# Strassen steps for both products of an MLP, in two passes with the activations in DRAM

## Chip, cores and metric

The kernel runs on one core of one Trainium2 chip. The metric is the device time of one execution in microseconds (us), as the median of a few runs. A profiled execution of the kernel before lies under the readings below.

## What is computed

Two transformer blocks over 1024 tokens of width 1024, in fp32. The change touches the end of the second: the last product with `w_out`, the norm, and the MLP.

```python
D_MODEL = 1024; SEQ = 1024; D_FF = 4 * D_MODEL
...
        x = x + jnp.einsum('bsd,de->bse', merged, w_out)

        h2 = rms_norm(x, norm2_g)
        u = jnp.square(jax.nn.relu(jnp.einsum('bsd,df->bsf', h2, w_up)))
        x = x + jnp.einsum('bsf,fd->bsd', u, w_down)
```

## The kernel before

TensorE takes fp32r operands, so every fp32 operand is split into a high part (a copy to fp32r) and a low part (the operand less its high part). A product is then three passes, high by high, high by low and low by high (`three_passes`, L202 issues all matmuls). The splits are work of the other engines: ScalarE (ACT) writes high parts, VectorE (DVE) the low parts of activations, GpSimd (POOL) the low parts of weights.

Each phase is a block with its own instruction stream for each engine, written out by hand and held together by semaphores; all engines pass a barrier between two blocks. There is no scheduler: every engine takes its instructions in the order of the code, and one that waits holds up all behind it. `phase_norm("n3", ...)` makes the last product with `w_out`, adds the residual into `res`, norms each of the 8 token tiles, turns it (transposes on TensorE) and leaves the turned rows in `a_hi` and `a_lo` (feature by token). Two halves of the first MLP units are also done there (`fm_half`).

`phase_mlp` takes the 4096 hidden features in 8 groups of 512. Of each group, `up` makes the four tiles of 128 features (8 k-tiles by two token halves by three passes, 48 matmuls of 128x512 each). ACT applies relu and square (`evacuate`) into `mlp_u`. The product with `w_down` of the group is one Strassen step: 512 rows of `w_down` by 1024 columns in four quadrants, and seven products `m1` to `m7` in place of eight. DVE makes the sums of activations (`total`, L2335) and their low parts (L2324), POOL the sums of weights (`combine`, L2147) and their low parts (`low`, L2154), ACT the high parts (`high` L2259, `w_part` L2262). A product has 4 token tiles of 6 matmuls, and DVE adds each tile from PSUM (`ps`) to one or two places of the residual in `res` (`add`, L2342). Products of one group and `up` tiles of the next are interleaved on TensorE:

```python
                        product(i, "m3", count("m3"), None if first else i * 28 - 4)
                        if not last:
                            pe.wait_ge(w_ready, ready(i, "up0"))
                            up(i + 1, 0)
                        product(i, "m4", count("m4"), i * 28)
                        product(i, "m5", count("m5"), i * 28 + 4)
```

All of `mlp_u` stays in SBUF. The weights of the next group are loaded by SP as soon as POOL has made the last low part that reads the buffer (`load_down`, `load_up`).

Of the kernel before, what the change touches and what calls it, by code (L numbers as in the profile page):

```python
# [13 lines left out]
P = 128  # L14
T = 1024
# [39 lines left out]
def program(nc, io, out):  # L55
    ctx = ExitStack()
    with ctx:
# [10 lines left out]
        x1 = dram("x1_tm", (T, D))  # L68
        qkv2 = dram("qkv2_tm", (T, 3072))
# [137 lines left out]
        n_mm_l, n_out_l, n_mm_r, n_prepared = (Tally(sem(n)) for n in ("n_mm_l", "n_out_l", "n_mm_r", "n_prepared"))  # L207
        n_added, n_normed, n_turned = (Tally(sem(n)) for n in ("n_added", "n_normed", "n_turned"))
# [1134 lines left out]
        def phase_norm(name, out_start, opened, x_src, gain, post_gain=None, x_dst=None, next_dst=None, next_col=0):  # L1343
# [12 lines left out]
            stored = n_stored if x_dst is not None else None  # L1356
            with ExitStack() as mem, nc.Block() as block:
# [11 lines left out]
                gain_in, chain, squared = S("gain_in"), S("chain"), S("squared")  # L1369
                rooted = S("rooted")  # L1370
# [119 lines left out]
                def _(act):  # L1490
                    passed = [0]

                    def square(src, total):
                        if passed[0]:
                            act.wait_ge(squared, passed[0])
                        nc.scalar.activation(junk[:, 0:src.shape[-1]], src, ACT.Square, accum_out=total).then_inc(squared, 1)
                        passed[0] += 1

# [55 lines left out]
                def _(dve):  # L1554
# [63 lines left out]
                    else:  # L1618
# [5 lines left out]
                        for s in range(NT + 1):  # L1624
                            if s < NT:
                                right_add(s)
                                pre_norm(s)
                            if s:
                                low(s - 1)

            for tally, n in ((n_hi, NT), (n_lo, NT), (n_mm_l, 2 * NT), (n_out_l, NT), (n_mm_r, NT), (n_prepared, NT),
# [410 lines left out]

        def phase_mlp():
# [11 lines left out]
            start = W_MLP[0][0]  # L2055
            u0, c0 = fm_units[0], tm_chunks[0]
            GROUPS = 8
            PRODUCTS = ("m3", "m4", "m5", "m2", "m1", "m6", "m7")
            STEPS = ("m3", "up0", "m4", "m5", "up1", "m2", "m1", "m6", "m7", "up2", "up3")
            QUARTER = {"up2": 0, "up3": 1, "m3": 2, "up0": 3, "m4": 0, "m5": 1, "up1": 2, "m2": 3, "m1": 0, "m6": 1, "m7": 2}  # L2060
            ADDS = {"m1": ((0, 0, ALU.add), (1, 1, ALU.add)), "m2": ((1, 0, ALU.add), (1, 1, ALU.subtract)),
                    "m3": ((0, 1, ALU.add), (1, 1, ALU.add)), "m4": ((0, 0, ALU.add), (1, 0, ALU.add)),
                    "m5": ((0, 0, ALU.subtract), (0, 1, ALU.add)), "m6": ((1, 1, ALU.add),), "m7": ((0, 0, ALU.add),)}
            OPERANDS = [("m3", 0), ("m3", 1)] + [(p, 0) for p in ("m4", "m5", "m2", "m1", "m6", "m7")] + \
                       [(p, 1) for p in ("m4", "m5", "m2", "m1", "m6", "m7")]
            SUMS = [(p, k) for k in range(2) for p in ("m5", "m2", "m1", "m6", "m7")]

            def tiles(p):
                return 4 * PRODUCTS.index(p)

            with ExitStack() as mem, nc.Block() as block:
                ut = sb(mem, "mlp_u", [P, 4, T])
                uo_hi = sb(mem, "mlp_uo_hi", [P, 7, 2, 512], F32R)
                uo_lo = sb(mem, "mlp_uo_lo", [P, 7, 2, 512], F32R)
                raw_b = sb(mem, "mlp_raw_b", [P, KB // 2, 512])
                raw_x = sb(mem, "mlp_raw_x", [P, 2, 512])
                raw_a = halved(w_raw)
                squared, u_hi, u_lo, summed = sem("mlp_squared"), sem("mlp_u_hi"), sem("mlp_u_lo"), sem("mlp_summed")
                a_in, b_in, x_in = sem("mlp_a_in"), sem("mlp_b_in"), sem("mlp_x_in")
                combined, w_high, w_ready = sem("mlp_combined"), sem("mlp_w_high"), sem("mlp_w_ready")  # L2080
                mm_d, ev_d = sem("mlp_mm_d"), sem("mlp_ev_d")

                r11, r21, r12, r22 = raw_a[:, 0:2, :], raw_a[:, 2:4, :], raw_b[:, 0:2, :], raw_b[:, 2:4, :]
                raw_of = {"m3": r12, "m4": r21, "m5": r22, "m2": r11, "m1": r22, "m6": r12, "m7": r21}

                def quarter(side, step):
                    q = QUARTER[step]
                    return halved(side[slot_of(start + 1 - q // 2)])[:, q % 2 * 2:q % 2 * 2 + 2, :]

                def by_k(tile):  # L2090
                    return tile.rearrange("p a (b n) -> p (a b) n", n=P)

                def u_part(p, k):

                    unit = k if p in ("m3", "m6", "m2") else 2 + k
                    half = 0 if p in ("m3", "m5", "m7") else 1
                    return ut[:, unit, half * 512:(half + 1) * 512]

                def ready(i, step):
                    return i * len(STEPS) + (STEPS.index(step) + 1)  # L2100

                def ready_last(step):
                    return (GROUPS - 1) * len(STEPS) + (PRODUCTS.index(step) + 1)

# [7 lines left out]
                def _(sp):  # L2112
                    def load_down(i, c):
                        rows = io["w_down_2"][i * 512:(i + 1) * 512, c * 512:(c + 1) * 512].rearrange("(k p) n -> p k n", p=P)
                        sp.dma_start((raw_b if c else raw_a)[:, :, :], rows).then_inc(b_in if c else a_in, 16)

                    def load_up(i, q):
                        col = i * 512 + q * P
                        sp.dma_start(by_k(raw_x[:, :, :]),
                                     io["w_up_2"][:, col:col + P].rearrange("(k p) n -> p k n", p=P)).then_inc(x_in, 16)  # L2120

                    load_down(0, 1)
                    for i in range(GROUPS - 1):
                        if i:
                            sp.wait_ge(w_ready, ready(i - 1, "up3"))
                        load_up(i + 1, 0)
                        sp.wait_ge(w_ready, ready(i, "up0"))
                        load_up(i + 1, 1)
                        sp.wait_ge(w_ready, ready(i, "up1"))
                        load_up(i + 1, 2)  # L2130
                        sp.wait_ge(w_ready, ready(i, "m7"))
                        load_down(i + 1, 1)
                        load_down(i + 1, 0)
                        sp.wait_ge(w_ready, ready(i, "up2"))
                        load_up(i + 1, 3)
                    for r, c, p in ((0, 1, "m5"), (1, 0, "m2"), (1, 1, "m6"), (0, 0, "m7")):
                        for t in range(4):
                            sp.wait_ge(ev_d, (GROUPS - 1) * 28 + tiles(p) + t + 1)
# [319 lines left out]
```

## Time and profile before

| quantity | before |
|---|---|
| median of 3 runs | 2311.85 us (2310.8 to 2312.58) |
| profiled execution, own time | 2313.34 us |
| its span, first to last instruction | 2311.6 us |
| mean granted TensorE clock | 0.993 of full |
| TensorE busy | 2233.6 us, 97% |
| GpSimd busy | 941.1 us, 41% |
| VectorE busy | 1319.2 us, 57% |
| ScalarE busy | 802.0 us, 35% |

Busy shares say how much of the span an engine had an instruction in work. A matmul's own duration in the trace overlaps its neighbours', so the pace is read from the distance of starts. Idle time in brackets names the engine or transfer that ended it.

### The profile page before, as it was taken

To read this page: it belongs to the slowest core of one execution; us is meant where nothing else is said; L and a number is where in the kernel's file an instruction comes from. 1 tells how busy PE (TensorE), PEld (TensorE's weight loads), DVE (VectorE), ACT (ScalarE), POOL (GpSimd) and SP (SyncE) were. 2 spreads that over 40 slices of the span, in tenths; PEclk is the share of its full clock that TensorE was granted. 3 is DMA by queue.
4 is the path that set the end of the run, shared out by engine and by line. 5 is a ranking of instruction groups with operands and counts; after the bars stand their busy time and mean duration, and the time that the engine had idled before them with its cause. 6 is when DMAs were issued, how large, how long until landed. Compare 5 with 4: busy or idle time off the path is not lost. (4 is left out here: it accounts for less than half of the span.)

```text
span 2311.6 us, 30049 instructions
## 1 busy us (share of the span) xinstructions
PE 2233.6 (97%) x10722; PEld 1854.4 (80%) x10722; DVE 1319.2 (57%) x2544; ACT 802.0 (35%) x1491; POOL 941.1 (41%) x732
## 2 busy tenths in 40 slices
PE   7999989999999999999999999999999999999997
PEld 7778777778877888888888788888888888888886
DVE  6666674516444666666666582334365565556467
ACT  5444424200004555555554131212333323323322
POOL 3232445535542322313313364553356355554534
PEclk9999999999999999999999999999999999999999
DMA  6220114212324323323322472222110110110211
GB/s 216 94 75 19 42 55 162 83 65 89 111 97 132 107 79 92 100 66 104 87 82 83 164 254 92 92 100 92 55 55 28 64 63 18 64 64 22 68 46 73
DMA packets 177605, 199.79 MB, mean 86 GB/s; under 512 B 56360, under 2 KB 126536, under 8 KB 177520
## 3 DMA queue, kind: packets, MB, share of 16 engines
q1 hardware_dynamic: 100352, 122.47, 16.1%
q10 hardware_dynamic: 77168, 76.19, 10.6%
q8 instruction: 53, 0.87, 0.2%
q14 instruction: 32, 0.26, 0.0%
HBM read 156.63 MB, written 50.40 MB: 90 GB/s over the span
## 5 line engine op out<-in xcount | busy, mean ns | idle before, releaser
L157 POOL TENSOR_TENSOR w_hi<-w_raw,zero 128x512 fp32r<-128x512 f32 x224 | 271.3, 1241 | 967.3 <-PE ps L202 847.5
L202 PE MATMUL ps<-a_hi,w_hi 128*128 128x512 f32 x1664 | 606.7, 405 | 7.4 <-PEq L1654 3.3
L202 PE MATMUL ps<-a_hi,w_lo 128*128 128x512 f32 x1664 | 586.8, 393 | 0.0
L202 PE MATMUL ps<-a_lo,w_hi 128*128 128x512 f32 x1664 | 584.7, 392 | 0.0
L202 PEld LDWEIGHTS ps<-a_hi,w_lo 128*128 128x128 f32 x1664 | 313.8, 189 | 69.3
L202 PEld LDWEIGHTS ps<-a_hi,w_hi 128*128 128x128 f32 x1664 | 314.8, 189 | 62.5 <-issue 9.2
L202 PEld LDWEIGHTS ps<-a_lo,w_hi 128*128 128x128 f32 x1664 | 315.2, 189 | 53.4
L2342 DVE TENSOR_TENSOR res<-res,ps 128x512 f32<-128x512 f32 x384 | 244.7, 682 | 118.0 <-PE ps L202 108.6
L162 POOL TENSOR_TENSOR w_lo<-w_raw,w_hi 128x512 fp32r<-128x512 f32 x224 | 299.7, 1370 | 4.4
L202 PE MATMUL ps<-w_hi,a_hi 128*128 128x512 f32 (+1 forms) x640 | 245.7, 384 | 7.5 <-PEq L1123 2.2
L202 PE MATMUL ps<-w_hi,a_lo 128*128 128x512 f32 (+1 forms) x640 | 244.1, 381 | 0.0
L202 PE MATMUL ps<-w_lo,a_hi 128*128 128x512 f32 (+1 forms) x640 | 244.0, 381 | 0.0
L202 PE MATMUL ps<-w_hi,mlp_uo_hi 128*128 128x512 f32 x448 | 179.1, 400 | 8.2 <-issue 5.4
L2324 DVE TENSOR_TENSOR mlp_uo_lo<-mlp_u,mlp_uo_hi 128x512 fp32r<-128x512 f32 x112 | 89.1, 829 | 160.8 <-ACT mlp_uo_hi L2259 159.1
L202 PE MATMUL ps<-w_lo,mlp_uo_hi 128*128 128x512 f32 x448 | 178.8, 399 | 0.0
L202 PE MATMUL ps<-w_hi,mlp_uo_lo 128*128 128x512 f32 x448 | 178.7, 399 | 0.0
L1894 ACT ACTIVATE prob<-prob,st 128x640 f32<-128x640 f32 (+4 forms) x128 | 89.3, 697 | 223.9 <-DVE st L2003 223.0
L202 PEld LDWEIGHTS ps<-w_hi,a_hi 128*128 128x128 f32 x640 | 121.7, 190 | 31.9 <-issue 7.5
L2154 POOL TENSOR_TENSOR w_lo<-w_raw,w_hi 128x512 fp32r<-128x512 f32 x48 | 62.5, 1324 | 203.1 <-ACT w_hi L2262 202.7
L202 PEld LDWEIGHTS ps<-w_hi,a_lo 128*128 128x128 f32 x640 | 121.9, 190 | 23.1
L202 PEld LDWEIGHTS ps<-w_lo,a_hi 128*128 128x128 f32 x640 | 121.9, 191 | 22.8
L532 DVE COPY stage_tm<-ps 128x512 f32<-128x512 f32 x40 | 27.7, 692 | 152.0 <-PE ps L202 152.0
(206 smaller groups left out, 3301.9 us busy)
## 6 DMA issues: line engine op xcount, KB each, us to landing
w_raw<-in_w_in_dram SPq DMA_DIRECT2D x32, 1024.0 KB, 5.2
feat_fm<-stage ACTq DMA_DIRECT2D x68, 256.0 KB, 2.1
mlp_raw_x<-in_w_up_dram SPq DMA_DIRECT2D x28, 512.0 KB, 4.1
conv_in<-feat_fm ACTq DMA_DIRECT2D x24, 512.0 KB, 5.8
qkv_tm<-stage_tm ACTq DMA_DIRECT2D x5, 2048.0 KB, 6.9
res<-in_x_dram SPq DMA_DIRECT2D x16, 512.0 KB, 6.4
w_raw<-in_w_out_dram SPq DMA_DIRECT2D x8, 1024.0 KB, 5.0
qk_raw<-qkv_tm ACTq DMA_DIRECT2D x32, 256.0 KB, 3.9
```

The costliest lines, as they stand in the source:

```text
L157: hi = nc.gpsimd.tensor_tensor(w_hi[slot][:, k:k + 2, :], w_raw[:, k:k + 2, :], zero[:, 0:1].unsqueeze(2).to_broadcast([P, 2, CW]), ALU.add)
L162: lo = nc.gpsimd.tensor_tensor(w_lo[slot][:, k:k + 2, :], w_raw[:, k:k + 2, :], w_hi[slot][:, k:k + 2, :].bitcast(F32), ALU.subtract)
L202: last = nc.tensor.matmul(out_of(o), lhs, rhs(o), start=first and n == 0, stop=final and n == 2)
L532: nc.vector.tensor_copy(stage[:, q, t, :], ps[:, t, 0:width]).then_inc(ev_tm, per)
L1894: nc.scalar.activation(prob[:, s, 0:w], prob[:, s, 0:w], ACT.Exp, scale=-1.0, bias=st[:, s, 1:2], accum_out=st[:, s, 2:3]).then_inc(exped, 1)
L2154: last = nc.gpsimd.tensor_tensor(quarter(w_lo, step)[:, k, :], raw[:, k, :], quarter(w_hi, step)[:, k, :].bitcast(F32), ALU.subtract)
L2324: nc.vector.tensor_tensor(uo_lo[:, int(p[1]) - 1, k, :], u_part(p, k), uo_hi[:, int(p[1]) - 1, k, :].bitcast(F32), ALU.subtract).then_inc( ...
L2342: last = nc.vector.tensor_tensor(rows, rows, ps[:, 4 + t, :], op)
```

## The change

The MLP becomes two passes. First all 8 groups of `w_up` are done, each as one Strassen step (seven products of 2 tiles by 12 matmuls, `up_tile`); the partial results are put together in `mlp_acc` by ACT (copies) and DVE (adds), ACT applies relu and square, and a DMA writes them to `u_fm` in DRAM. The residual also passes through DRAM (`x2`). Then the product with `w_down` is done in 4 groups of 1024 hidden features, seven products of 4 tiles by 12 matmuls each, in the order m5, m3, m2, m1, m6, m4, m7. The activation quadrants of a product are loaded from `u_fm`, summed by DVE and split two products ahead of their use. The seven operands of the first pass are made once: two are parts of the normed rows, two are differences made in the new `phase_norm_last`, three are sums made by POOL there.

The new phase between the product with `w_out` and the MLP, at each token tile t:

```diff
+                    for t in range(4, NT):
+                        pool.wait_ge(n_hi.sem, hi0 + t + 1)
+                        toks = slice((t - 4) * P, (t - 3) * P)
+                        nc.gpsimd.tensor_tensor(raw_c[:, :, toks], turned_row(t - 4, 0), turned_row(t, 4), ALU.add).then_inc(p_sum, 1)
+                        nc.gpsimd.tensor_tensor(turned_row(t - 4, 4), turned_row(t - 4, 4), turned_row(t, 4), ALU.add).then_inc(p_sum, 1)
+                        pool.wait_ge(u_sum, t + 1)
+                        nc.gpsimd.tensor_tensor(turned_row(t, 0), turned_row(t, 0), turned_row(t - 4, 0), ALU.add).then_inc(p_sum, 1)
...
+                    def low(t):
...
+                        nc.vector.tensor_tensor(diff[:, t % 2, :, :], turned_row(t, k0), turned_row(t, k1), ALU.subtract).then_inc(u_sum, 1)
...
+                    for s in range(NT + 2):
+                        if s < NT:
+                            right_add(s)
+                            pre_norm(s)
+                        if 1 <= s <= NT:
+                            low(s - 1)
+                        if s >= 2:
+                            diff_low(s - 2)
```

The first pass on TensorE, one product:

```diff
+        def up_tile(p, fb, last=False):
...
+            for k in range(4):
+                mm = three_passes(lambda _: ps[:, 2 * UP_PLACE[p] + fb, :], wh[:, k, cols], wl[:, k, cols],
+                                  lambda _: high[:, k, :], lambda _: low[:, k, :], (0,), k == 0, k == 3)
```

The second pass, SP (loads of weights), POOL, TensorE, ACT and DVE in turn; `s` counts the 28 products:

```diff
+                        if p == "m6":
+                            sp.wait_ge(w_ready, NU + s + 1)
+                            load_down(g, 1, 0)
...
+                            if p == "m7":
+                                sp.wait_ge(combined, down_sum(s))
+                                load_down(g + 1, 1, 1)
+                                sp.wait_ge(w_ready, NU + s + 1)
+                                load_down(g + 1, 0, 1)
...
+                    for s in range(ND):
+                        g, p = s // 7, DOWN[s % 7]
...
+                        if p == "m1":
+                            pool.wait_ge(a_in, 16 * GROUPS + 16 * (g + 1))
+                            down_total(r1, r1, r2, ALU.add)
+                        if p == "m6":
+                            pool.wait_ge(combined, down_sum(s) - 1)
+                            down_total(r0, r0, r1, ALU.add)
+                        if p == "m4":
+                            pool.wait_ge(b_in, 16 * GROUPS + 32 * g + 32)
+                            down_total(r0, r0, r2, ALU.subtract)
...
+                        pool.wait_ge(w_high, NU + s + 1)
+                        for k in range(4):
+                            ins = nc.gpsimd.tensor_tensor(down_slot(w_lo, s)[:, k, :], raw_of[p][:, k, :],
+                                                          down_slot(w_hi, s)[:, k, :].bitcast(F32), ALU.subtract)
+                        ins.then_inc(w_ready, 1)
...
+                    for s in range(ND):
+                        pe.wait_ge(w_ready, NU + s + 1)
+                        pe.wait_ge(u_lo, SPLIT_UP + 4 * s + 4)
...
+                        for t in range(4):
...
+                                pe.wait_ge(ev_p, 8 * GROUPS + 4 * (s - 2) + t + 1)
+                            toks = slice(t * P, (t + 1) * P)
+                            for k in range(4):
+                                mm = three_passes(lambda _: ps[:, 4 * (s % 2) + t, :], high[:, k, toks], low[:, k, toks],
...
+                    for s in range(ND):
+                        if s + 1 < ND:
+                            act.wait_ge(mm_p, NU + 4 * s)
+                            down_high(s + 1)
+                        if s + 2 < ND:
+                            staged_high(s + 2)
...
+                    for s in range(ND):
+                        if s + 2 < ND:
+                            staged_sum(s + 2)
...
+                        for t in range(4):
+                            down_add(s, t)
+                            if s + 2 < ND and t < 2:
+                                staged_low(s + 2, (2 * t, 2 * t + 1))
```

`down_total` and `staged_sum` are four `tensor_tensor` of 128x512, `down_high` is two copies of 128x1024, `staged_high` and `staged_low` are four instructions of 128x512. `down_high` of five of the seven products waits for `combined`, which `down_total` raises; the weight parts alternate between two slots.

**POOL, the last group's weights.** In the program of before, in the last group of 512 features, the low parts for m3, m4 and m5 stand together, and then the sums for m1, m6 and m7 (x2 is two instructions alike):

```order
L2154 TENSOR_TENSOR w_lo1<-mlp_raw_b,w_hi1 128x512 [waits mlp_w_high]
L2154 TENSOR_TENSOR w_lo1<-mlp_raw_b,w_hi1 128x512
L2154 TENSOR_TENSOR w_lo0<-w_raw,w_hi0 128x512 [waits mlp_w_high]
L2154 TENSOR_TENSOR w_lo0<-w_raw,w_hi0 128x512
L2154 TENSOR_TENSOR w_lo0<-mlp_raw_b,w_hi0 128x512 [waits mlp_w_high]
L2154 TENSOR_TENSOR w_lo0<-mlp_raw_b,w_hi0 128x512
L2147 TENSOR_TENSOR mlp_raw_b<-w_raw,mlp_raw_b 128x512 x2
L2147 TENSOR_TENSOR mlp_raw_b<-mlp_raw_b 128x512 [waits mlp_combined]
```

In the changed program, in the first group of the second pass, from the sum for m6 to the low part for m7:

```order
L2532 TENSOR_TENSOR mlp_raw_b<-mlp_raw_b,mlp_raw_c 128x512 [waits mlp_combined]
L2532 TENSOR_TENSOR mlp_raw_b<-mlp_raw_b,mlp_raw_c 128x512 x3
L2555 TENSOR_TENSOR w_lo1<-mlp_raw_b,w_hi1 128x512 [waits mlp_w_high]
L2555 TENSOR_TENSOR w_lo1<-mlp_raw_b,w_hi1 128x512 x3
L2532 TENSOR_TENSOR mlp_raw_b<-mlp_raw_b,w_raw 128x512 [waits mlp_b_in]
L2532 TENSOR_TENSOR mlp_raw_b<-mlp_raw_b,w_raw 128x512 x3
L2555 TENSOR_TENSOR w_lo0<-mlp_raw_b,w_hi0 128x512 [waits mlp_w_high]
L2555 TENSOR_TENSOR w_lo0<-mlp_raw_b,w_hi0 128x512 x3
```

A sum and the low part that is made of it now stand directly behind one another, four instructions each, with a wait for ACT (`mlp_w_high`) between them and a wait for a load (`mlp_b_in`) ahead of m4's sum.

**DVE, one product.** Before, a product's adds (two for each token tile), with two low parts of the next group ahead of the next product's adds (register arithmetic left out):

```order
L2342 TENSOR_TENSOR res<-res,ps 128x512 [waits mlp_mm_d]
L2342 TENSOR_TENSOR res<-res,ps 128x512
...
L2324 TENSOR_TENSOR mlp_uo_lo<-mlp_u,mlp_uo_hi 128x512 [waits mlp_u_hi]
```

In the changed program, one product of the second pass with sums two products ahead (`mlp_part_x` and `mlp_part_y` are the loaded quadrants):

```order
L2748 TENSOR_TENSOR mlp_part_y<-mlp_part_x,mlp_part_y 128x512 [waits row_in0]
L2748 TENSOR_TENSOR mlp_part_y<-mlp_part_x,mlp_part_y 128x512 x3
L2799 TENSOR_TENSOR res<-res,ps 128x512 [waits mlp_ev,mlp_mm]
L2799 TENSOR_TENSOR res<-res,ps 128x512
L2753 TENSOR_TENSOR a_lo<-mlp_part_y,a_hi 128x512 [waits mlp_u_hi] x2
```

Four sums now stand ahead of a product's adds and four low parts between them (two behind the first tile's adds, two behind the second's), eight instructions that read two operands in SBUF.

## Rows read from the trace of the kernel before

**Rows 1.** The page, busy time, share of the span and instructions of each engine.

```profile
PE 2233.6 (97%) x10722; PEld 1854.4 (80%) x10722; DVE 1319.2 (57%) x2544; ACT 802.0 (35%) x1491; POOL 941.1 (41%) x732
```

**Rows 2.** Busy us in stretches: PE, PEld, DVE, ACT, POOL, granted clock, DMA share, GB/s.

```profile
1759.00:1841.60 82.60, 82.60 (x361) 67.46 (x360) 48.68 (x72) 27.98 (x33) 42.21 (x32) 1.00 0.16 51
```

**Rows 3.** Line 202 from 1590 us: count, ns min/median/max, first and last start.

```profile
L202 PE MATMUL ps<-a_hi,w_hi x512: 389/389/477, 1631.0 to 2254.6; 128*128 128x512 f32 x171
L202 PE MATMUL ps<-w_hi,mlp_uo_hi x448: 392/394/767, 1676.1 to 2307.1; 128*128 128x512 f32 x150
```

**Rows 4.** The chain that ended last, in order of time: start us, us, what.

```profile
1643.38 612.53 PE ps L202 x2664
...
2264.33 12.99 PE ps L202 x48
...
2278.48 2.96 POOL w_lo L2154 x2
...
2282.68 25.26 PE ps L202 x96
```

**Rows 5.** Timeline of DVE: adds behind 12 matmuls, then behind 6.

```profile
1566.67 0.69 DVE L1560 TENSOR_TENSOR res<-ps,res 128x512 f32<-128x512 f32 x1 [1.94 <-PE ps L202]
...
1569.39 0.69 DVE L1560 TENSOR_TENSOR res<-ps,res 128x512 f32<-128x512 f32 x1 [1.91 <-PE ps L202]
...
1813.15 0.69 DVE L2342 TENSOR_TENSOR res<-res,ps 128x512 f32<-128x512 f32 x1 [0.71 <-PE ps L202]
1814.55 0.69 DVE L2342 TENSOR_TENSOR res<-res,ps 128x512 f32<-128x512 f32 x1 [0.71 <-PE ps L202]
```

**Rows 6.** Groups of instructions, 1759 to 2255 us: count, busy us, mean ns, idle before.

```profile
L2342 DVE TENSOR_TENSOR res<-res,ps 128x512 f32<-128x512 f32 x288 | 183.4, 682 | 94.7 <-PE ps L202 87.9
L2324 DVE TENSOR_TENSOR mlp_uo_lo<-mlp_u,mlp_uo_hi 128x512 fp32r<-128x512 f32 x84 | 68.4, 849 | 109.9 <-ACT mlp_uo_hi L2259 108.7
```

**Rows 7.** Timeline of POOL and DVE from 1788 us, both on SBUF operands.

```profile
1788.05 2.40 DVE L2335 TENSOR_TENSOR mlp_u<-mlp_u 128x512 f32<-128x512 f32 x2
1788.06 3.55 POOL L2154 TENSOR_TENSOR w_lo<-mlp_raw_b,w_hi 128x512 fp32r<-128x512 f32 x2 [3.03 <-ACT w_hi L2262]
...
1790.37 2.39 DVE L2324 TENSOR_TENSOR mlp_uo_lo<-mlp_u,mlp_uo_hi 128x512 fp32r<-128x512 f32 x2
1792.69 1.28 DVE L2335 TENSOR_TENSOR mlp_u<-mlp_u 128x512 f32<-128x512 f32 x2
```

**Rows 8.** Timeline of POOL and DVE from 1766 us, DVE reading PSUM.

```profile
1766.14 4.86 DVE L2342 TENSOR_TENSOR res<-res,ps 128x512 f32<-128x512 f32 x8
...
1768.61 2.56 POOL L2147 TENSOR_TENSOR mlp_raw_b<-w_raw,mlp_raw_b 128x512 f32<-128x512 f32 x2
```

**Rows 9.** Timeline of ACT: two high parts of weights, 128x1024 each.

```profile
2258.63 1.05 ACT L2262 ACTIVATE w_hi<-w_raw 128x1024 fp32r<-128x1024 f32 x1
2259.58 1.04 ACT L2262 ACTIVATE w_hi<-mlp_raw_b 128x1024 fp32r<-128x1024 f32 x1
```

**Rows 10.** Timeline of POOL: a low part, a load into its source, the next high part.

```profile
1556.10 5.04 POOL L162 TENSOR_TENSOR w_lo_n<-w_raw,w_hi_n 128x512 fp32r<-128x512 f32 x4
1566.43 4.03 POOL L157 TENSOR_TENSOR w_hi<-w_raw,zero 128x512 fp32r<-128x512 f32 x4 [5.29 <-DMA w_raw<-in_w_out_dram]
```

**Rows 11.** Busy us in stretches, as rows 2, behind two idle times of TensorE.

```profile
2266.00:2268.00 2.00, 2.00 (x6) 1.62 (x5) 2.00 (x4) 0.00 (x0) 1.92 (x3) 0.51 0.00 0
2284.00:2286.00 2.00, 2.00 (x6) 1.52 (x6) 1.91 (x4) 2.00 (x3) 0.00 (x0) 0.50 0.00 0
```

**Rows 12.** Timeline of DVE in the norm, a token tile's pass.

```profile
1617.62 0.69 DVE L1564 TENSOR_TENSOR res<-ps,res 128x512 f32<-128x512 f32 x1 [1.11 <-PE ps L202]
...
1620.49 1.28 DVE L1599 SCALAR_TENSOR_TENSOR mt_n<-res,stat_n,gpre_n 128x1024 f32<-128x1024 f32 x1
1621.69 1.22 DVE L1604 TENSOR_TENSOR a_lo<-ps,a_hi 128x1024 fp32r<-128x1024 f32 x1
1624.02 0.69 DVE L1564 TENSOR_TENSOR res<-ps,res 128x512 f32<-128x512 f32 x1 [1.11 <-PE ps L202]
```

More of the change, by code:

```diff
@@ L68, in program @@
         x1 = dram("x1_tm", (T, D))
+        x2 = dram("x2_tm", (T, D))
+        u_fm = dram("u_fm", (4 * D, T))
         qkv2 = dram("qkv2_tm", (T, 3072))
@@ L2040, in _ @@
                     pair_loop(dve, body)
-        def phase_mlp():
[L2055 to L2069, printed above, removed]
-            with ExitStack() as mem, nc.Block() as block:
[L2072 to L2103, printed above, removed]
@@ L2143, in _, with up_low @@
                 @block.gpsimd
                 def _(pool):
-                    def combine(dst, a, b, op):
-                        for k in range(2):
+                    def up_low(i, p, last):
+                        pool.wait_ge(w_high, i * 7 + (UP.index(p) + 1))
+                        high, low = up_quarter(w_hi, p, last), up_quarter(w_lo, p, last)
+                        for k in range(0, 4, 2):
+                            ins = nc.gpsimd.tensor_tensor(low[:, k:k + 2, :], up_raw(p)[:, k:k + 2, :],
+                                                          high[:, k:k + 2, :].bitcast(F32), ALU.subtract)
+                        ins.then_inc(w_ready, 1)
@@ L2147, in combine, with body, down_total @@
+                    def body(i, first, last):
+                        for p in UP[2 if first else 0:]:
+                            up_low(i, p, last)
+                    periods(pool, body)
+                    def down_total(dst, a, b, op):
+                        for k in range(4):
                             last = nc.gpsimd.tensor_tensor(dst[:, k, :], a[:, k, :], b[:, k, :], op)
                         last.then_inc(combined, 1)
-                    def low(count, step):
-                        pool.wait_ge(w_high, count)
-                        raw = raw_of.get(step, raw_x)
-                        for k in range(2):
-                            last = nc.gpsimd.tensor_tensor(quarter(w_lo, step)[:, k, :], raw[:, k, :],
-                                                           quarter(w_hi, step)[:, k, :].bitcast(F32), ALU.subtract)
-                        last.then_inc(w_ready, 1)
@@ L2202, in product, with up @@
-                    def product(i, p, count, before):
-                        high, low, o = quarter(w_hi, p), quarter(w_lo, p), int(p[1]) - 1
-                        pe.wait_ge(w_ready, count)
-                        pe.wait_ge(u_lo, i * 14 + (OPERANDS.index((p, 1)) + 1))
+                    def up(i, p, last):
+                        pe.wait_ge(w_ready, i * 7 + (UP.index(p) + 1))
+                        for fb in range(2):
+                            mm = up_tile(p, fb, last)
+                        mm.then_inc(mm_p, 1)
@@ L2254, in high, with up_high @@
[L2254 to L2262 removed]
+                    def up_high(i, p, last=False):
+                        nc.scalar.activation(up_quarter(w_hi, p, last), up_raw(p), ACT.Copy).then_inc(w_high, 1)
@@ L2264, in body, with staged_high @@
+                    def staged_high(s):
+                        if s >= 2 and PARTS[DOWN[s % 7]][1] is None:
+                            act.wait_ge(*staged_in(s))
+                        for k in range(4):
+                            if PARTS[DOWN[s % 7]][1] is not None:
+                                act.wait_ge(u_sum, NT + summed[s] + k + 1)
+                            nc.scalar.activation(down_operand(a_hi, s)[:, k, :], total(s)[:, k, :], ACT.Copy).then_inc(u_hi, 1)
                     def body(i, first, last):
-                        def multiplied(p):
-                            return i * 28 + (tiles(p) + 4)
```

742 lines of the change are left out of this document (539 added, 203 removed).

## The prediction

> **What bounds the kernel now.** I read the page first: TensorE is in work for 97% of the span, POOL for 41% [rows 1]. Then the stretches: in a steady part of the MLP TensorE has no gap at all, DVE is in work for 59% of the time and POOL for 51% [rows 2]. The chain that ended last is one unbroken piece of 2664 matmuls up to the last group; only there do gaps come, where the chain goes over ACT, DVE and POOL [rows 4]. So the MLP is bound by the number of matmuls, and a change pays if it takes matmuls away and the other engines still keep up. The reader should carry both halves of that into what follows.
>
> **Matmuls taken away.** The MLP has 1536 matmuls in the first product and 1344 in the second [rows 3]. Adds behind units of 12 matmuls come 2.72 us apart, 0.2267 us for each matmul; behind 6 with a wait they come 1.40 us apart, so a tile's wait costs about 0.04 us [rows 5]. The first product takes 1536 x 0.2267 = 348.2 us, the second 224 x 1.40 = 313.6 us. The MLP runs from 1631.0 to 2308.0 us [rows 3, 4], 677 us; the rest, some 15 us, is the last turn, a few tenths between phases and the gaps of the last group. The change makes the first product 8 x 7 x 24 = 1344 matmuls, 304.7 us plus 2.2 us of waits = 306.9. The second has 28 products of 4 tiles of 12, at 2.76 us a tile: 11.04 us a product, 77.3 us a group, 309.1 us in all. With 1 us for the last turn that is 617 us, 60 us less than before, if TensorE never waits.
>
> **The first pass** keeps up. A group lasts 38.4 us. POOL has seven low parts of two instructions (about 18 us), DVE eight adds of 128x1024 (1.2 us each, two of the halves in [rows 8]) and five sums of two instructions, 16 us; ACT seven high parts, four copies and eight passes of 128x1024, at 0.95 to 1.05 us [rows 9], 20 us. The tightest step is m4's weights for the next group: their slot is free 5.5 us before the group ends, ACT and POOL need 3.6, and m4 runs 5.5 us into the next. I add nothing. Transfers are 4 MB a group, hidden; without that cover each late load would cost its 5.3 us.
>
> **Two engines on one resource.** Rows 7 decide the rest. DVE and POOL start together on SBUF operands at 1788.05. A DVE instruction that is alone takes 0.6 us (two in 1.28), a POOL one 1.25 (two in 2.56 [rows 8]). Here DVE's first two take 2.40 = 0.6 + 1.8 and the next two 2.39, POOL's two take 3.55 = 0.6 + 1.25 + 0.6 + 1.25 less a tenth: each instruction waits until the other engine's is over, and they alternate [rows 7]. When DVE adds from PSUM, eight take 4.86 us and POOL's two stay at 2.56 [rows 8], so adds don't take part. Over the steady part it shows in the means already, 849 ns for a low part against 682 for an add [rows 6]. The Trainium skill (SBUF — State Buffer, Who interferes with whom) says that a VectorE instruction with two SBUF inputs and a GpSimd one that reads SBUF lock each other out for the whole instruction, and one with a single SBUF input does not. It speaks against this change; by it the sum comes out as it does below from the rows, and if it did not hold, the sum would be that of batches without collisions.
>
> **The second pass.** A product needs four DVE low parts, five of seven four DVE sums: 48 instructions of 0.6 us a group, 28.8 us. POOL makes five sums and seven low parts of four: 48 of 1.25, 60 us. On one resource that is 88.8 us against TensorE's 77.3. But the order binds harder. For a product with a sum POOL does four instructions, ACT two high parts (0.95 each and 0.1 for the signals, 2.0 us [rows 9]), POOL four more, and POOL has nothing else to do while ACT works. For m4 a load into `mlp_raw_b` must also come between m6's low part and m4's sum: 1561.14 to 1566.43 in the same pattern, 5.3 us [rows 10].
>
> I walk one group; time 0 is the end of the preceding m7. POOL's sum for m3 is over at 1.5, its low part at 10.7 (ready for 11.0). m2's weight slot is free when m5 ends at 11.0, so from there the chain runs without slack: high part (2.0), low part m2, sum m1, high, low, sum m6, high, low, load (5.3), sum m4, high, low, sum m7, high, low. That is five high parts, nine batches of four POOL instructions and one load: 10.0 + 5.3 + nine batches. A batch alone is 5.05 us [rows 10]; each DVE instruction between adds 0.6. Stepping both engines by alternation, with DVE's order of sums, add, two low parts, add, two low parts, adds, I get the ends: low m2 19.8, sum m1 27.2, low m1 35.95, sum m6 43.35, low m6 51.5, load 56.8, sum m4 62.5, low m4 71.25, sum m7 78.65, low m7 87.4. So the nine batches take 61.1 us, 6.8 each, and 26 of the group's 48 DVE instructions fall into them. TensorE waits 2.9 us before m1, 4.5 before m6, 8.7 before m4 and 5.1 before m7, which ends at 98.4.
>
> Idle TensorE also loses its clock. Behind gaps of 2.8 and 5.4 us it is granted half, 1.2 instead of 2.4 GHz [rows 11], and 48 and 96 matmuls take 12.99 and 25.26 us instead of 11.2 and 22.4 [rows 4], 1.8 and 2.9 more. Behind m1, m6 and m4 the next wait absorbs this; behind m7 it counts, 2.2 us. The group is 100.6 us, 23.3 more than 77.3. Four groups: 93; the first starts its m3 about 2.5 later, the last has no sums for a following group and saves about 4.5. **+91 us.**
>
> Loads of activations (2 MB a product at most, a product and a half ahead) stay hidden behind the POOL chain; DVE, with 29 us of adds (48 of 0.61) and 29 of sums and low parts a group, plus its waits, lags by up to half a product, which the second PSUM set covers.
>
> **The phase between.** Per token tile DVE is free for 1.1 of 6.4 us now [rows 12]; the change halves `low` (-0.6) and adds two instructions of 0.6, leaving 0.5. POOL works on SBUF meanwhile, first on m2's and m4's weights (17 us), then three sums for each of the last four tiles; each collision costs DVE up to 1.25. I take 1.2 us on the first tiles, 2.2 at tiles 6 and 7. Behind the last turn ACT copies twice (1.7), POOL sums (about 5), the barrier follows, then ACT's high part (1.1) and POOL's low part of m5 (2.6): about 10.6 us, of which m4's 5.4 cover half, so TensorE waits 5.2, plus 2.0 for the clock. **+11 us**, bounds 3 and 16. The queue behind: all ACT copies of the first group follow that high part, with 8 us of slack.
>
> **Sum.** 617 + 11 + 91 = 719 us against 677: +42. The profiled execution would be 2313.3 + 42 = 2355; it lies 1.5 us above the median of 2311.85, so the median becomes 2354 us.
>
> **Rivals.** (A) The collisions hardly happen, because DVE falls into POOL's 15.3 us of waiting per group. Batches are 5.05, the chain 10 + 5.3 + 45.5, the group 82.9 and 2.2 for the clock; four groups +31. 617 + 11 + 31 = 659, 18 less than before: 2294 us, faster. For it: half of DVE's work is adds that don't collide. Against it: 48 instructions cannot fit in 15 us. It decides from below 89.9 us a group, where the time is that of before; that is 5.8 us a batch, some 11 collisions a group in place of 26. (B) POOL's chain isn't on the path at all, and the change gives its matmuls: 617 + 11, 2263 us. Against it is the count of 88.8 us on one resource. (C) Collisions are at their worst, four in each batch, 7.45 us: the group 10 + 5.3 + 67 + 22.1 + 2.2 = 106.7, four +118, total 746: 2381 us; late activation sums would come to the same. (D) Half the collisions, 5.95 a batch: the group 93.2, +64, total 692: 2327 us.
>
> **Numbers.** Forecast 0.52, D 0.14, C 0.13, A 0.12, B 0.04; 0.05 for a time within 0.2% between A and D. 0.2%, 4.6 us, is about what a measurement of this kernel can tell from no change. Faster 0.16 (A and B), same 0.05, slower 0.79. Cases of both signs: the forecast alone would range from 2335 to 2375; the range that leaves out A, B and the far end of C is 2305 to 2385.
>
> **What would show it.** Right: 2688 MLP matmuls; a first pass of about 307 us without gaps; in the second pass POOL near 80% in work, its 128x512 batches near 6.8 us, DVE instructions on `mlp_part` at up to 1.85 us each, groups of about 100 us, gaps on TensorE before m1, m6, m4 and m7 released by POOL's `w_lo`, the longest before m4 with a load of `mlp_raw_b` in it, and a granted clock clearly under 1. Wrong: groups under 90 us with POOL instructions at 1.25 (A), or gaps released by DVE or by loads of `u_fm`, which I take as hidden.

## The result, and the profile after

The changed kernel takes 2334.23 us (median of its four executions), the kernel before, run beside it, 2311.8 us (2310.8 to 2312.58). One of the four, of 4426 us, was disturbed: it is in the median of 2334.23 us but not in the ratio, and the three others took 2333.42 to 2334.99 us, with a median of 2333.48. The ratio is 1.0096, 95% interval 1.0076 to 1.0116: 22.4 us slower, where 42 were forecast. The profiled execution took 2334.99 us.

The head of the page: busy time by engine, share of the span and instructions (answers to [rows 1]).

```profile
span 2333.2 us, 29563 instructions
PE 2199.3 (94%) x10530; PEld 1825.2 (78%) x10530; DVE 1480.9 (63%) x2516; ACT 867.5 (37%) x1577; POOL 1094.8 (47%) x796
```

TensorE has 192 matmuls less and is in work for 34 us less, and the span is 21.6 us longer: 56 us more of idle time came in. Where that lies is told by TensorE's waits from 1500 us on: what it waited for, us in total, times, longest.

```profile
PE ps L204 <- POOL w_lo L2555: 56.4, 15, 8.4
PE ps L204 <- POOL w_lo L2521: 7.8, 2, 7.1
...
```

L2555 is the low part of weights in the second pass, L2521 the one in the first. In the kernel before there was no such wait in a steady stretch [rows 2]. The stretches of the changed kernel, columns as in [rows 2]: the start of the MLP, the first pass, the turn to the second with most of its first group, and two stretches as long as a group in the second.

```profile
1640.00:1655.00 15.00, 7.90 (x23) 6.03 (x22) 10.48 (x7) 10.35 (x15) 13.48 (x9) 0.66 0.00 0
1655.00:1946.00 291.00, 290.28 (x1273) 238.54 (x1273) 189.14 (x153) 152.70 (x157) 153.93 (x107) 1.00 0.39 130
1946.00:2032.50 86.50, 72.79 (x300) 58.60 (x298) 83.20 (x88) 28.77 (x40) 69.11 (x45) 0.92 0.61 218
2032.50:2128.60 96.10, 81.55 (x336) 65.79 (x336) 89.71 (x97) 30.06 (x44) 76.02 (x49) 0.95 0.49 175
2128.60:2224.70 96.10, 81.37 (x336) 65.61 (x336) 87.95 (x97) 29.77 (x43) 76.08 (x49) 0.95 0.50 175
```

The first pass has 0.7 us of gap in 291 at a granted clock of 1.00. In the second pass TensorE is idle for 14.6 us of each 96.1, and its clock is 0.95. The chain that ended last (start us, us, what) shows a whole group of the second pass, from the m7 of one group to that of the next:

```profile
2128.67 22.08 PE ps L204 x96
...
2150.77 2.02 ACT w_hi L2649 x2
...
2152.86 6.40 POOL w_lo L2555 x4
2159.26 7.00 POOL mlp_raw_c L2532 x4
...
2168.43 6.39 POOL w_lo L2555 x4
2174.82 7.00 POOL mlp_raw_b L2532 x4
...
2183.99 5.95 POOL w_lo L2555 x4
...
2189.95 5.24 DMA mlp_raw_b<-in_w_down_dram
...
2195.26 5.63 POOL mlp_raw_b L2532 x4
...
2203.36 6.34 POOL w_lo L2555 x4
2209.70 6.32 POOL mlp_raw_b L2532 x4
...
2218.19 6.52 POOL w_lo L2555 x4
...
2224.76 22.07 PE ps L204 x96
```

Between two pieces of 96 matmuls (m7 and the next group's m5) the chain goes over nine POOL batches, five pairs of ACT high parts (2.0 us each, most left out here) and one load: the chain that the prediction walked, link by link. What is new against it is the length of the batches, 5.6 to 7.0 us with a mean of 6.4, where it had 5.7 to 7.4 with a mean of 6.8. Taken one by one, 26 of the 36 POOL instructions in these nine batches last 1.7 to 1.9 us; the other ten last 1.3.

The timeline of DVE over two of these batches (start us, us, what; in brackets the idle time before):

```profile
2153.15 6.66 DVE L2748 TENSOR_TENSOR mlp_part_y<-mlp_part_x,mlp_part_y 128x512 f32<-128x512 f32 x4
2159.73 1.27 DVE L2799 TENSOR_TENSOR res<-res,ps 128x512 f32<-128x512 f32 x2
2160.93 2.38 DVE L2753 TENSOR_TENSOR a_lo<-mlp_part_y,a_hi 128x512 fp32r<-128x512 f32 x2
2163.23 1.27 DVE L2799 TENSOR_TENSOR res<-res,ps 128x512 f32<-128x512 f32 x2
2164.43 2.38 DVE L2753 TENSOR_TENSOR a_lo<-mlp_part_y,a_hi 128x512 fp32r<-128x512 f32 x2
```

Two adds from PSUM take 1.27 us as before [rows 8]. Two low parts, both operands in SBUF, take 2.38, as in [rows 7], and four sums 6.66 instead of about 2.5. A batch of four POOL instructions that meets four of DVE's takes 7.00 us, one alone 5.05 [rows 10]: a meeting costs POOL 0.49 us, where 0.6 was assumed.

TensorE's clock just behind the gap before m4 (columns as above), and its timeline at the first matmul of m4 and of m7:

```profile
2113.00:2119.00 6.00, 5.32 (x13) 4.17 (x14) 6.00 (x6) 0.00 (x0) 6.00 (x5) 0.50 0.00 0
```

```profile
2113.68 0.80 PE L204 MATMUL ps<-w_hi,a_hi 128*128 128x512 f32 x1 [6.53 <-POOL w_lo L2555]
...
2128.67 0.50 PE L204 MATMUL ps<-w_hi,a_hi 128*128 128x512 f32 x1 [1.25 <-POOL w_lo L2555]
```

Behind the gap of 2.4 us before m1 the 48 matmuls take 11.2 us, the full pace; behind that of 3.9 us before m6 they take 12.8, and behind that of 6.5 us before m4 13.7.

### The profile page after: what moved, and what is told of

Its sections match the earlier page's. It is cut to its first block and busy times, and to the rows that moved or that the text cites. A ratio compares the mean times of both kernels' runs of the same rounds, so it can differ in the third digit from the quotient of the medians.

```text
span 2333.2 us, 29563 instructions
## 1 busy us (share of the span) xinstructions
PE 2199.3 (94%) x10530; PEld 1825.2 (78%) x10530; DVE 1480.9 (63%) x2516; ACT 867.5 (37%) x1577; POOL 1094.8 (47%) x796
## 5 line engine op out<-in xcount | busy, mean ns | idle before, releaser
L204 PE MATMUL ps<-w_hi,a_hi 128*128 128x512 f32 (+1 forms) x1088 | 428.0, 393 | 63.9 <-POOL w_lo L2555 56.4
L204 PE MATMUL ps<-w_lo,a_hi 128*128 128x512 f32 (+1 forms) x1088 | 424.2, 390 | 0.0
L204 PE MATMUL ps<-w_hi,a_lo 128*128 128x512 f32 (+1 forms) x1088 | 424.2, 390 | 0.0
L204 PEld LDWEIGHTS ps<-w_hi,a_hi 128*128 128x128 f32 x1088 | 209.8, 193 | 113.4 <-POOL w_lo L2555 62.8
L204 PEld LDWEIGHTS ps<-w_hi,a_lo 128*128 128x128 f32 x1088 | 209.3, 192 | 42.2
L204 PEld LDWEIGHTS ps<-w_lo,a_hi 128*128 128x128 f32 x1088 | 209.7, 193 | 40.9
L2799 DVE TENSOR_TENSOR res<-res,ps 128x512 f32<-128x512 f32 x192 | 121.4, 675 | 16.7 <-PE ps L204 16.7
L2521 POOL TENSOR_TENSOR w_lo<-mlp_raw_b,w_hi 128x512 fp32r<-128x512 f32 x60 | 85.4, 1446 | 98.2 <-ACT w_hi L2615 98.2
L2019 DVE TENSOR_TENSOR pt_lo<-ps,pt_hi 128x512 fp32r<-128x512 f32 (+1 forms) x192 | 87.9, 485 | 44.8 <-ACT pt_hi L1909 44.8
L2555 POOL TENSOR_TENSOR w_lo<-mlp_raw_b,w_hi 128x512 fp32r<-128x512 f32 x64 | 99.2, 1581 | 36.5 <-ACT w_hi L2649 36.5
L2753 DVE TENSOR_TENSOR a_lo<-mlp_part_y,a_hi 128x512 fp32r<-128x512 f32 x76 | 98.5, 1335 | 22.1 <-ACT a_hi L2658 22.1
```

Source lines behind the costliest of these rows:

```text
L204: last = nc.tensor.matmul(out_of(o), lhs, rhs(o), start=first and n == 0, stop=final and n == 2)
L2019: ins = nc.vector.tensor_tensor(pt_lo[:, sl:sl + cnt, cols], ps[:, bank, 0:cnt * P].rearrange("p (j n) -> p j n", n=P), pt_hi[:, sl:sl + c ...
L2521: ins = nc.gpsimd.tensor_tensor(low[:, k:k + 2, :], up_raw(p)[:, k:k + 2, :], high[:, k:k + 2, :].bitcast(F32), ALU.subtract)
L2555: ins = nc.gpsimd.tensor_tensor(down_slot(w_lo, s)[:, k, :], raw_of[p][:, k, :], down_slot(w_hi, s)[:, k, :].bitcast(F32), ALU.subtract)
L2753: nc.vector.tensor_tensor(down_operand(a_lo, s)[:, k, :], total(s)[:, k, :], down_operand(a_hi, s)[:, k, :].bitcast(F32), ALU.subtract).th ...
L2799: last = nc.vector.tensor_tensor(rows, rows, ps[:, 4 * (s % 2) + t, :], op)
```

## The experiments

Eleven kernels were run in three sets: runs 1 to 4, 5 to 8, and 9 to 11. Beside them the kernel before took 2312.45, 2311.37 and 2313.03 us. Kernels that leave work out were run once, the others four to eight times.

**1. DVE's instructions on SBUF taken away, 2. DVE's adds taken away, 3. POOL's work taken away.** Each is a width of 8 columns in place of 512, in the second pass only. Runs 1 and 3 do the same to the low parts.

```diff
-    nc.vector.tensor_tensor(y[:, k, :], x[:, k, :], y[:, k, :], op)
+    nc.vector.tensor_tensor(y[:, k, 0:8], x[:, k, 0:8], y[:, k, 0:8], op)
...
-    last = nc.vector.tensor_tensor(rows, rows, ps[:, 4 * (s % 2) + t, :], op)
+    last = nc.vector.tensor_tensor(rows[:, 0:8], rows[:, 0:8], ps[:, 4 * (s % 2) + t, 0:8], op)
...
-    last = nc.gpsimd.tensor_tensor(dst[:, k, :], a[:, k, :], b[:, k, :], op)
+    last = nc.gpsimd.tensor_tensor(dst[:, k, 0:8], a[:, k, 0:8], b[:, k, 0:8], op)
```

> In the second pass DVE's sums and low parts of activations work on 8 columns in place of 512, so that the low parts are stale; every wait, ACT, POOL and TensorE stay as they are. Theory (DVE and POOL exclude each other on SBUF operands): POOL's batches of four fall from a mean of 6.4 us to 5.05, the group from 96.1 to 22.1 + 10.9 + 5.3 + 45.5 = 84 us, and the time to about 2286 us. Rival (POOL's batches are long for another reason, ACT's or the transfers' traffic): batches stay at 6.4 us and the time at 2334 us.

> In the second pass DVE's adds from PSUM work on 8 columns in place of 512 (the output is incomplete), sums and low parts stay. Theory: adds with one operand in PSUM take no part in the collisions and DVE is not the bound, so batches stay between 6 and 7 us and the time within 6 us of 2334. Rival 1 (any DVE instruction slows POOL): batches fall, the time falls by 20 us or more. Rival 2 (DVE, in work for 93% of a group, is itself the bound): the group falls from 96 towards 80 us, the time to about 2275.

> In the second pass POOL's sums and low parts of weights work on 8 columns in place of 512 (weights' low parts are stale). Theory: nothing else holds TensorE, 28 products take 309 us in place of 381, and the time is about 2262 us, 50 less than before the change: what the fewer matmuls give less the phase between. Rival (activation loads, ACT or DVE come next behind POOL): gaps remain, the time is 2285 us or more.

Run 1 took 2292.57 us, run 2 2335.68, run 3 2259.88: the theory holds in each, and run 1 lies 7 us above its figure. Run 1's POOL timeline over one load:

```profile
2154.72 5.11 POOL L2555 TENSOR_TENSOR w_lo<-mlp_raw_b,w_hi 128x512 fp32r<-128x512 f32 x4 [2.18 <-ACT w_hi L2649]
2164.93 5.04 POOL L2532 TENSOR_TENSOR mlp_raw_b<-mlp_raw_b,w_raw 128x512 f32<-128x512 f32 x4 [5.09 <-DMA mlp_raw_b<-in_w_down_dram]
2172.43 5.01 POOL L2555 TENSOR_TENSOR w_lo<-mlp_raw_b,w_hi 128x512 fp32r<-128x512 f32 x4 [2.47 <-ACT w_hi L2649]
```

Every batch is back at 5.0 to 5.1, the waits of POOL for ACT and for the load are unchanged, and the group is 85.0 us instead of 96.1. So the meetings with DVE are worth 11 us of each group, 42 of the 2334 us. They would be worth a little more if nothing took the chain's place: nine batches of 5.05 us would make a group of 84.0, but in run 1 only the gap before m4 is left, and the chain goes over m4, m7 and the next m5 and seven batches:

```profile
2177.50 35.47 PE ps L204 x144
```

These 144 matmuls stand behind a gap of 5.9 us and take 35.5 us; at the pace of 22.08 us for 96 they would take 33.1.

In run 2, taking away DVE's other work, the adds, changes nothing, though DVE's busy time falls from 88 to 70 us of 96.1: it is not DVE's load, it is which of its instructions stand beside POOL's. In run 3, without POOL's work, TensorE has no gap in the second pass and full clock (1.00), and the time is 52.6 us less than that of the kernel before: the 60 us of matmuls less the start's loss are really there to be had.

**4. The load off the chain.** m4's quadrant of `w_down` gets a buffer of its own in `mlp_acc`, which is free in the second pass, and is loaded from m2 on.

```diff
...
-                raw_of = {"m5": r1, "m3": r0, "m2": r2, "m1": r1, "m6": r0, "m4": r0, "m7": r0}
+                raw_of = {"m5": r1, "m3": r0, "m2": r2, "m1": r1, "m6": r0, "m4": r3, "m7": r3}
...
```

> The quadrant of w_down for m4 and m7 gets a buffer of its own (memory that is free in the second pass), loaded two products earlier; the computation is complete. Theory: the load's 5.2 us leave the chain of each of the four groups, the group is 91 us and the time about 2313 to 2318 us (POOL then waits less, so a few more collisions). Rival (the load lies beside other work): 2334 us.

It took 2319.22 us (2315.71 to 2321.81), ratio to before 1.0031 (1.0020 to 1.0042): 15 us of the 22 are gone, and the median lies 1 us above the theory's range. The groups, from m7 to m7, are 90.6, 91.7 and, the last, 88.6 us; the chain is nine batches, five highs and 96 matmuls, without a load. Its stretch, columns as above:

```profile
2128.60:2224.70 96.10, 86.27 (x364) 69.78 (x363) 95.91 (x104) 30.79 (x43) 80.38 (x51) 0.96 0.54 193
```

DVE now has hardly any idle time left: the same work takes place in a shorter group.

**5. POOL's next sum ahead of its low part.** POOL waited 2.2 us for ACT between each sum and the low part made of it. With a second buffer the next product's sum fills that wait.

```diff
...
+                    for s in range(ND):
+                        if s + 1 < ND:
+                            sums(s + 1)
+                        p = DOWN[s % 7]
                         pool.wait_ge(w_high, NU + s + 1)
```

> As e4_buffer, and POOL makes the sum for the next product ahead of the low part of this one (m7's sum goes to a further buffer), so that ACT's high part is made while POOL works; the computation is complete. Theory 1 (the order on POOL is what is left): the five waits of 2.18 us go, the group falls from 90.3 to the 84 us that the instructions of both engines on SBUF need one after another, and the time from 2319 to about 2295 us. Theory 2 (DVE, which has no idle time left in e4_buffer, is now a bound of its own, since each of its waits on POOL is its own time): the group stays at 87 us or more, the time at 2308 to 2319 us.

It took 2301.65 us (2299.19 to 2302.85), ratio 0.9959 (0.9944 to 0.9973): 10 us faster than the kernel before, and the only order of work so far that makes the change pay. The group is 85.8 us. The time lies between the two theories (2295, and 2308 to 2319): the group came near what the first gave, and yet DVE has become a bound. The same two stretches, and a part of its chain:

```profile
2032.50:2128.60 96.10, 89.98 (x385) 72.73 (x384) 96.10 (x110) 34.58 (x49) 88.58 (x55) 0.98 0.58 201
2128.60:2224.70 96.10, 89.31 (x383) 72.42 (x383) 96.10 (x106) 33.14 (x47) 88.54 (x55) 0.98 0.58 205
```

```profile
2144.91 2.39 DVE res L2809 x4
2147.30 3.04 DVE mlp_part_y L2758 x3
2150.34 0.89 issue
2151.23 1.78 DVE mlp_part_y L2758
2153.01 0.73 DVE res L2809 x2
2154.13 1.28 DVE a_lo L2763 x2
```

TensorE's waits still name POOL's `w_lo`, 29.2 us. But in the steady groups the chain goes over DVE from end to end: POOL waits for ACT's `w_hi`, and ACT, which takes its instructions in order, stands at `a_hi` waiting for DVE's sums (100.2 us in the 192 us of the two stretches). The engine that TensorE waits for is two steps away from the one that is late.

**6. The gap at the start.** The first high and low parts of m5 and m3 are made inside the norm's block, and the sums of the last two token tiles go behind the barrier.

```diff
-                    for t in range(4, NT):
+                    for t in range(4, 6):
...
+                    for n, p in ((3, "m5"), (4, "m3")):
+                        pool.wait_ge(w_high, n)
...
```

> Only the start of the first pass differs: ACT and POOL split m5's and m3's first weights inside the norm's block, and POOL makes the operand sums of the last two tiles behind the barrier; the computation is complete. Theory (the 7.1 us gap before the first m5 is the barrier, one high part and one low part behind POOL's sums): the gap and some 1.5 us of half clock go, 2334 becomes about 2326 us. Rival (POOL's sums are late for m1's operands instead, the gap moves): 2331 us or more.

It took 2333.81 us (2331.54 to 2333.95), no change that can be measured, as the rival said. TensorE's waits from 1500 us:

```profile
PE ps L204 <- POOL w_lo L2575: 56.6, 15, 8.6
PE ps L204 <- POOL w_lo L2532: 3.8, 3, 1.9
PE ps L204 <- DVE mlp_op_lo L2750: 1.7, 1, 1.7
...
```

The gap of 7.1 us is gone, and four smaller ones of 0.5 to 1.9 stand in its place. POOL makes the sums of two token tiles behind the barrier now, and what comes after them is late: its low parts for m1 and for the next group, and DVE's low part of m6's operand.

**7. The version of run 5 with DVE's SBUF instructions small, 8. with its adds small** (the edits of runs 1 and 2 on top of run 5's).

> e5_ahead with DVE's sums and low parts of the second pass on 8 columns (the low parts are stale). Theory: with no collisions POOL needs 60 us of a 77 us group and nothing waits, the time is that of e3_small_pool, 2260 us. Rival (POOL's order or its latency still binds by itself): above 2275 us.

> e5_ahead with DVE's adds of the second pass on 8 columns (the output is incomplete). DVE has 29 us a group less to do, the instructions that meet POOL are as many. If DVE's own time is the bound in e5_ahead, the group falls by 3 us or more against e5_ahead and the time by 12 us or more; if POOL with its collisions is the bound, the time stays within 5 us of e5_ahead.

The first took 2261.53 us, as the theory had it, with a granted clock of 1.00 and no gap in the steady groups. The second took 2300.72, within 1 us of run 5, although DVE now has 9 to 10 us of idle time in 96.1. Its groups are 84.2 and 85.8 us, and its chain is back on POOL:

```profile
2146.78 6.80 POOL mlp_raw_b L2537 x4
2153.58 6.82 POOL w_lo L2565 x4
2160.41 6.79 POOL mlp_acc L2537 x4
```

Each of these batches meets four DVE instructions. So taking work off DVE alone gives nothing: a chain over POOL of the same length takes the place of the one over DVE, stretched by the same thing. The likely reason is the sum on the one resource, which is reckoned and not shown by a run of its own: a pair of one POOL and one DVE instruction takes 1.70 to 1.75 us, 48 pairs 82 to 84 us, and the group of run 5 is 85.8.

**9. Longer instructions on POOL, 10. on both engines.** If only the sum of time on the shared resource counted, it would not matter in what pieces it is taken.

```diff
...
-                        for k in range(4):
-                            last = nc.gpsimd.tensor_tensor(dst[:, k, :], a[:, k, :], b[:, k, :], op)
+                        for k in range(0, 4, 2):
+                            last = nc.gpsimd.tensor_tensor(dst[:, k:k + 2, :], a[:, k:k + 2, :], b[:, k:k + 2, :], op)
...
```

The low parts are changed in the same way.

> The version with POOL's next sum ahead (2301.65 us), in which POOL's sums and low parts of the second pass are 24 instructions of 128x1024 a group in place of 48 of 128x512. In the trace of before one of 128x1024 takes 2.40 us, two of 128x512 2.50. Theory 1, the sum of both engines' time on one resource decides and who holds it how long does not: POOL's busy time falls by 48 x 0.05 = 2.4 us a group, the group from 85.8 to about 83.5, four groups -9: 2291 to 2297 us. Theory 2, turns decide: the engines take turns, and there are only 24 POOL instructions to take turns with, so at most two DVE instructions fall into a batch in place of four. A POOL batch would be at most 4.8 + 2 x 0.5 = 5.8 us in place of 7.0, and a DVE instruction waits up to 2.4 us in place of 1.25. DVE, with hardly any idle time already, then falls behind: groups above 87 us, TensorE waits for a_lo or for DVE's adds, not for w_lo, 2305 to 2330 us.

> As the run with wide POOL instructions, and DVE's sums and low parts of the second pass are 128x1024 too, 24 a group of 1.22 us in place of 48 of 0.6. Theory 1 (the sum of times on the one resource decides): as with POOL alone wide, 2291 to 2297 us. Theory 2 (turns decide): the engines alternate evenly again, a collision costs POOL about 1.1 us and DVE 2.4, the same per element as before; what is saved is handovers, so 2290 to 2300 us, clearly below the run in which POOL alone is wide. The two runs differ by over 8 us by theory 2 and by under 3 by theory 1.

POOL alone wide took 2330.52 us (2329.3 to 2331.86), ratio 1.0075 (1.0058 to 1.0091): 29 us slower than run 5, just beyond the far end of what the theory of turns gave (2305 to 2330), and far outside the other (2291 to 2297). POOL's and DVE's timeline in one product, and what ACT waited for in 192 us:

```profile
2156.98 5.20 POOL L2565 TENSOR_TENSOR w_lo<-w_raw,w_hi 128x1024 fp32r<-128x1024 f32 x2 [7.39 <-ACT w_hi L2659]
2162.15 5.19 POOL L2537 TENSOR_TENSOR mlp_raw_b<-mlp_raw_b,mlp_raw_c 128x1024 f32<-128x1024 f32 x2
2172.34 5.18 POOL L2565 TENSOR_TENSOR w_lo<-mlp_raw_c,w_hi 128x1024 fp32r<-128x1024 f32 x2 [5.00 <-ACT w_hi L2659]
```

```profile
2157.86 4.87 DVE L2763 TENSOR_TENSOR a_lo<-mlp_part_y,a_hi 128x512 fp32r<-128x512 f32 x2
2162.66 2.47 DVE L2809 TENSOR_TENSOR res<-res,ps 128x512 f32<-128x512 f32 x4
2165.05 4.65 DVE L2758 TENSOR_TENSOR mlp_part_y<-mlp_part_x,mlp_part_y 128x512 f32<-128x512 f32 x4
```

```profile
ACT a_hi L2668 <- DVE mlp_part_y L2758: 129.6, 18, 16.3
```

POOL's batches fell from 6.0 to 7.0 us to 5.2 to 6.1, and half of them stand behind idle times of 3 to 9 us; two DVE low parts take 4.87 us instead of 2.38, since each waits for the end of a POOL instruction of 2.4. DVE has no idle time, its chain is the longest one, and the group is 93.5 us. The whole loss is DVE's: the durations of its 48 instructions on SBUF operands add up to 68.5 us a group, where they add up to 60.8 in run 5, and the group has grown by as much (93.5 against 85.8). In one thing the expectation was wrong: TensorE still waits for `w_lo` (48.5 us), over the detour by ACT.

With both wide the time is 2303.79 us (2303.38 to 2304.9), ratio 0.9958 (0.9942 to 0.9975): turns are even again and the 27 us are back. Next to nothing is saved on handovers: a pair of wide instructions starts 3.34 to 3.39 us behind the one before, two narrow pairs take 3.40 to 3.44. The group is 86.9 to 87.3 us against 85.8, and the time lies above both ranges, by 4 us above the nearer.

**11. Run 5 with the start of run 6.**

> The version with POOL's next sum ahead (2301.65 us) and the changed start of the first pass (0.4 us less than the changed kernel by itself) in one kernel. Theory 1, the start's gap only moves: 2300 to 2303 us. Theory 2, the gap's 5 us come back now that less waits behind it: 2294 to 2298 us.

It took 2300.98 us (2298.24 to 2303.67), ratio 0.9941 (0.9924 to 0.9958). That is run 5 within what can be measured, as theory 1 had it, so the start's 7 us are not to be had by moving them, here either. The two times are the best that were found.

## Why the prediction was right in kind and too large in size

**Matmuls and first pass: right.** The second pass begins at 1948.4 us; the prediction's terms up to there, 1631.0 + 306.9 + 11, give 1948.9. That the 11 us came out is luck in part, for its parts did not. The gap before m5 was 7.1 us in place of 5.2, and behind it 14 matmuls took 6.0 us in place of 3.2, 2.9 us of lost clock where 2.0 were taken. Against that, the 3.4 us for DVE's longer steps never reached TensorE: the step is 7.45 us at the last tiles, about as reckoned, against 6.4 before [rows 12], yet TensorE's first MLP matmul lies at 1629.6, 1.4 us earlier than before. Run 3 bears out the sum without waits: 2259.88 against the 2263 of rival B.

**The mechanism of the second pass: right.** The chain is nine batches, five highs, one load, with the gaps where they were said to be in a steady group, before m1, m6, m4 and m7, released by `w_lo`, the longest before m4 (6.5 to 8.4 us). Runs 1 and 2 show that it is the SBUF instructions of DVE and not its adds. The rule of the Trainium skill (SBUF — State Buffer, Who interferes with whom), that a VectorE instruction with two SBUF inputs and a GpSimd one reading SBUF contend, while one with a single SBUF input does not, agrees: 6.66 us for four sums, 1.27 for two adds. That the lock holds for the whole instruction, as the prediction has it from there, is not borne out to the tenth: alternating pairs start 1.70 to 1.72 us apart, where 0.6 and 1.25 make 1.85.

**The size of a group: the step that failed.** It was 100.6 by the prediction and is 96.1.

| term of a group | predicted | measured |
|---|---|---|
| nine POOL batches | 61.1 | 57.6 |
| five pairs of high parts with signals | 10.0 | 11.1 |
| load of m4's quadrant | 5.3 | 5.3 |
| m7 and the next m5 | 22.1 | 22.1 |
| half clock behind m7's gap | 2.2 | 0 |

First, "each DVE instruction between adds 0.6": it added less. The trace has 26 lengthened POOL instructions in the chain of a group, and 26 were walked; (57.6 - 9 x 5.05) / 26 is 0.47 us for each, 0.49 in a batch that meets four. The count was right and the price too high by a fifth. The 0.6 was taken as a whole DVE instruction's time. The rows already had the right price: POOL's two instructions take 3.55 us where both meet DVE [rows 7] and 2.56 where none does [rows 8], 0.5 for each. The prediction noted a tenth less than its four terms and did not use it.

Second, "behind m7 it counts, 2.2 us": the gap before m7 was 1.25 us in place of 5.1, and the matmuls behind it ran at full pace (22.08 us for 96, not 25.26 as in [rows 4]). Behind m4's gap of 6.5 us the clock was 0.50, and the 48 matmuls of m4 took 2.6 us more than at full pace. The prediction says that the next wait absorbs this, but it left that wait, m7's, at 5.1 us. Between the first matmuls of m4 and m7 lie 15.0 us where 16.15 were walked, so the shorter batches took 1.2 us off the gap before m7, and m4's slow matmuls the other 2.6. Where that gap is longer the clock does count: in run 4 it was once 4.2 us, and the 96 matmuls behind it took 23.57 us.

```profile
2119.34 23.57 PE ps L204 x96
```

Over the four groups: 95.7, 95.6, 96.1 and 94.2 us (from the start at 1948.4 and the ends of m7 at 2044.1, 2139.7, 2235.8 and 2330.1) against 103.1, 100.6, 100.6 and 96.1. That is 18.8 us of the 20 by which the forecast was too high. In the first group m3 did come late, by 3.1 us where 2.5 were forecast, but the chain goes over m2's low part, and that ended 8.9 us behind m5 in place of 8.5 in a steady group; so only 0.4 us of it counted. The last group saved 1.9 us, not 4.5.

**Rivals.** Rival A (DVE falls into POOL's waits) is out by the count of 26 meetings. Its time for the case without collisions, 2294, is close to run 1's 2292.6, and so is its group, 85.1 against 85.0; but it had nine batches and a clock lost at m7, and in run 1 the chain goes over seven batches and the clock is lost at m4, so the agreement is luck in part. Its line on where it decides leaves out its own 2.2 us for the clock: at 89.9 us a group a batch is 5.6 us, not 5.8, and the meetings are 8, not 11. Nothing else hangs on that. Rival B is out by TensorE's waits for `w_lo`, and rival C by the batches: no more than two of a group's nine met DVE four times, at 7.0 us and not 7.45. Rival D's group of 93.2 lay nearer in time (2327) than the forecast, and it would have been right for a wrong reason: not half the meetings, but all of them at a lower price.

**What stays open.** Why a meeting costs POOL less than 0.5 us when DVE's instruction takes 0.6 alone isn't settled; the two evidently overlap by 0.1 to 0.15 us, and no run shows on which side. That the wide version of both engines is 1 to 1.5 us a group longer than the narrow one was measured, not explained.

## What to carry to other kernels

Before trading matmuls for sums on other engines, walk the chain of one product through them: here 60 us of matmuls were won and the waits with the slower matmuls behind them, most of them on one chain over POOL, ACT and a load, gave back 82; a buffer more and a sum made one product early (runs 4 and 5) turned the loss of 22 us into a gain of 10. Where VectorE and GpSimd both work on SBUF operands, count pairs and not busy times, price a pair from a row in which both meet, and be wary of making the instructions of one engine longer than the other's; here that cost 29 us. And when TensorE waits for one engine, follow the chain to its end before making that engine faster: in run 5 the name in TensorE's waits and the engine that was late were different ones.

## What the runs showed that was not expected

- Instruction length decides who loses more on the shared resource, in the one unequal case that was run: POOL at 128x1024 against DVE at 128x512 moved most of the delay to DVE and cost 29 us; both at 128x1024 and both at 128x512 are 2 us apart.
- A pair of 128x512 instructions, one on each engine, takes 1.70 to 1.75 us, less than 0.6 + 1.25.
- A gap of 1.25 us of TensorE left its clock at full speed although it had been at half (0.50) behind a gap of 6.5 us some ten microseconds earlier.
